# First modulation by feature tiles with three QKV units abreast; later modulation in two norm passages, last head turned inside the output projection, bias loads on SP

## Chip, cores and metric

The kernel runs on one core of one Trainium2 chip. The time is that of one execution on the device, in microseconds; of several runs the median counts.

## What is computed

Two blocks one after the other on 256 tokens of width 1024, in float32. Only the first block is touched here. It has two layers and a second stream of 256 context tokens that passes through the first layer too.

```python
silu_c, silu_cc = jax.nn.silu(c), jax.nn.silu(c_ctx)
for i in range(DEPTH):                       # DEPTH = 2
    sh1, sc1, g1, sh2, sc2, g2 = jnp.split((silu_c @ ada_w[i] + ada_b[i])[:, None, :], 6, axis=-1)
    csh1, csc1, cg1, csh2, csc2, cg2 = jnp.split(silu_cc @ ada_w[i] + ada_b[i], 6, axis=-1)
    h  = rmsnorm(x,  norm_mix[i]) * (1.0 + sc1)  + sh1
    hc = rmsnorm(xc, norm_mix[i]) * (1.0 + csc1) + csh1
    y, yc = diff_attention(...) if i == 0 else neighbourhood_attention(...)
    x = x + g1 * y
    h2 = rmsnorm(x, norm_ffn[i]) * (1.0 + sc2) + sh2
    x = x + g2 * conv_ffn(h2, ...)           # and the same for xc in layer 0
```

`ada_w[i]` is 1024 x 6144: 24 MB a layer, all of it read to multiply two vectors. `diff_attention` subtracts two softmaxes for each of 8 heads, normalizes each head and projects; `neighbourhood_attention` adds a table of relative biases (`rpb`) to the scores.

## The kernel before

**Layout.** Features lie on the 128 partitions, in 8 tiles of 128; both streams stand side by side, 512 columns a tile (`X`, 256 in layer 1 where only x is left). A product is taken in three float32r parts: operands are split into a high and a low half, and `mm3` (line 516) issues high x high, high x low, low x high. A normalized tile is `NH` and `NL`, a weight unit `WH` and `WL`.

**The weight stream.** All weights come as units of up to 1 MB, in the order of the list KEYS that `unit_orders` (line 143) writes out: ("qkv", l, i), ("wo", l, i), ("up", l, j), ("down", l, c, m) and so on. SP issues them in that order (`load_unit`, line 468) into three buffers `RAW`, unit v into v % 3; a load waits until unit v - 3 has been used. `split_hi` (ACT, two halves) writes `WH`, `split_lo` (VectorE or POOL, two halves, by POOL_EVERY) writes `WL`; `ahead` names the unit that is two further in the split order. Every engine runs its own instructions in the order written.

**Modulation.** A block ("ada", b, k), b from 0 to 5, is 2048 columns of the six vectors of a layer, so three blocks a layer; k runs over the 8 feature tiles of the contraction. `pe_ada` (line 523) multiplies silu(c) and silu(c_ctx) (`CB`) with one 1 MB unit, unsplit, in four products into bank `AB`; the sum is there after all eight k. Then `act_ada_row` copies the bank, `pe_ada_turn` transposes it and `dve_ada` adds the bias into `ADA`; `dve_gain` makes the gains `AMOD`. Block 0 (shift and scale of layer 0) is done at the start. Block 1 is spread over the eight QKV units, one before each; block 2 over the four V units; block 3 over the first eight up units of layer 0; block 4 over the first down units; block 5 over the second half of the up units.

**The norm.** Squares, `pe_sums` (products with a column of ones; POOL adds the first six tiles ahead in `pool_presum`), `dve_mean`, `pool_rsqrt`, the broadcast `pe_rs_rows`, and then tile by tile `dve_scale`, `act_norm` (writes `NH`; shifts a copy for odd tiles) and the low half on VectorE (even tiles) or POOL (odd ones).

**Start, in order.** SP loads SMALL, unit 0, CONST, unit 1, X in two halves with units 2 and 3 between. PE runs block 0 with the sums between, the broadcast, the turn. Then the first QKV unit runs with all its tiles' eight k steps.

**Attention of layer 0** (`pe_diff` and its three siblings) runs 43 steps; in step n job n (a head and a quarter of the queries) does its QK, and older jobs their later stages: exponential at age 1, mix at 3 (`POOL_MIX` names those on POOL), transposes at 4, PV at 5, and for every fourth job the head's norm at ages 8 and 9 on POOL (L1062, L1067), the turn on PE at 10 (L941), `NH` and `NL` of the head at 11. ACT and POOL split wo(0,0) in steps 1 and 2, ACT and VectorE wo(0,1) in step 35. `pe_wo` follows.

**Attention of layer 1** (`pe_na`, 22 steps, pairs p): scores, bias and maximum on VectorE, exponentials on ACT (L1166), scale on POOL (L1200), transposes and PV. The biases of a chunk of four pairs are loaded into `BR` by four DMAs of 256 KB (`act_load_bias`), then POOL writes `BI` from them in two additions (`pool_bias`, L1102). ACT issues chunk 2 in step 4 and chunk 3 in step 8, among its own work.

## Time and profile before

| what | value |
|---|---|
| median of 3 runs | 1737.33 us (1736.33 to 1737.52) |
| the profiled execution | 1738.02 us, its span 1736.1 us |
| PE busy | 1629.7 us, 94% of the span |
| VectorE, ACT, POOL busy | 868.5, 741.3, 540.7 us |
| HBM read | 246.63 MB, 143 GB/s over the span |

### The profile page before, as it was taken

The page shows a single profiled execution, that of the slowest core. Times are in us where ns is not written, and L with a number is a line of the kernel's source. Part 1 is how long each engine was busy: PE and PEld are TensorE (multiplying, and loading weights), DVE is VectorE, ACT ScalarE, POOL GpSimd, SP SyncE. Part 2 cuts the span into 40 slices and gives each one's busy share as a digit, 9 for nine tenths or more (in the row PEclk, how much of TensorE's full clock was granted, in tenths as well). Part 3 has the DMA queues.
Part 4 walks back from the last instruction along what each step waited for, and adds up shares of the span by engine and source line. Part 5 has one row for each costly group of instructions (what it writes and reads, how often), then busy time and mean ns, then how long its engine had stood idle before and what let it go on. Part 6 is the DMA issues. An engine that isn't in the chain of part 4 may idle for free.

```text
span 1736.1 us, 26371 instructions
## 1 busy us (share of the span) xinstructions
PE 1629.7 (94%) x10864; PEld 1414.9 (81%) x10864; DVE 868.5 (50%) x1367; ACT 741.3 (43%) x1332; POOL 540.7 (31%) x362
## 2 busy tenths in 40 slices
PE   4999876999999999989978999999999999999997
PEld 1778654877777777878955899999999998999997
DVE  2642376345532355343145588747466454568434
ACT  2421376243422233333246555534654444554442
POOL 2321244222211122211326111104433555523553
PEclk9999999989999999989989999999999999999998
DMA  8543500234436344324321455454534553633551
GB/s 337 182 182 127 213 1 25 73 140 152 155 128 238 116 152 156 99 81 136 138 83 26 149 175 190 145 196 139 191 122 154 186 170 116 214 122 122 184 185 45
DMA packets 52903, 249.38 MB, mean 144 GB/s; under 512 B 20656, under 2 KB 21680, under 8 KB 26288
## 3 DMA queue, kind: packets, MB, share of 16 engines
q1 hardware_dynamic: 36000, 242.32, 39.7%
q10 hardware_dynamic: 16784, 5.38, 1.4%
q8 instruction: 86, 1.41, 0.3%
q14 instruction: 33, 0.27, 0.0%
HBM read 246.63 MB, written 1.05 MB: 143 GB/s over the span
## 4 chain that ended last, share of the span: by engine, by line
PE 88%; DVE 4%; POOL 3%; issue 2%; ACT 1%; DMA 1%; SPq 0%; POOLq 0%; DVEq 0%; ACTq 0%
PE psq L518 20%; PE psq L519 19%; PE psq L520 19%; PE ps L518 6%; PE ps L520 6%; PE ps L519 6%; PE ps L531 3%; DMA RAW<-wstream 1%; DVE STAT L1019 1%; PE psq L969 1%; PE psq L1835 1%; PE ps L626 1%; PE ps L668 1%; PE ps L1126 1%; PE psq L1139 1%
## 5 line engine op out<-in xcount | busy, mean ns | idle before, releaser
L518 PE MATMUL psq<-NH,WH 128*128 128x256 f32 (+1 forms) x1904 | 602.4, 316 | 20.1 <-POOL NL L2159 5.9
L519 PE MATMUL psq<-NL,WH 128*128 128x256 f32 (+1 forms) x1904 | 594.2, 312 | 0.0
L520 PE MATMUL psq<-NH,WL 128*128 128x256 f32 (+1 forms) x1904 | 593.6, 312 | 0.0
L500 DVE TENSOR_TENSOR WL<-RAW,WH 128x1024 fp32r<-128x1024 f32 (+2 forms) x265 | 315.8, 1216 | 459.9 <-ACT WH L490 459.9
L500 POOL TENSOR_TENSOR WL<-RAW,WH 128x1024 fp32r<-128x1024 f32 (+2 forms) x115 | 288.0, 2506 | 597.5 <-ACT WH L490 597.4
L490 ACT ACTIVATE WH<-RAW 128x1024 fp32r<-128x1024 f32 (+2 forms) x380 | 361.2, 1001 | 221.4 <-DMA RAW<-wstream 177.7
L518 PEld LDWEIGHTS psq<-NH,WH 128*128 128x128 f32 x1904 | 369.7, 194 | 59.8 <-issue 27.1
L520 PEld LDWEIGHTS psq<-NH,WL 128*128 128x128 f32 x1904 | 369.9, 194 | 18.7
L519 PEld LDWEIGHTS psq<-NL,WH 128*128 128x128 f32 x1904 | 370.2, 194 | 17.7
L1414 POOL TENSOR_TENSOR HL<-TMP,HH 128x512 fp32r<-128x512 f32 (+1 forms) x44 | 45.5, 1033 | 247.8 <-ACT HH L1343 134.1
L518 PE MATMUL ps<-NH,WH 128*128 128x256 f32 (+1 forms) x368 | 122.5, 333 | 0.0
L520 PE MATMUL ps<-NH,WL 128*128 128x256 f32 (+1 forms) x368 | 121.9, 331 | 0.0
L519 PE MATMUL ps<-NL,WH 128*128 128x256 f32 (+1 forms) x368 | 121.8, 331 | 0.0
L588 ACT ACTIVATE TMP<-X 128x256 f32<-128x256 f32 (+1 forms) x52 | 24.8, 496 | 154.5 <-DVE X L1233 112.0
L518 PEld LDWEIGHTS ps<-NH,WH 128*128 128x128 f32 x368 | 70.4, 191 | 12.1 <-issue 5.0
L520 PEld LDWEIGHTS ps<-NH,WL 128*128 128x128 f32 x368 | 70.4, 191 | 6.5
L519 PEld LDWEIGHTS ps<-NL,WH 128*128 128x128 f32 x368 | 70.3, 191 | 6.2
L1392 DVE SCALAR_TENSOR_TENSOR TMP<-psq,SMALL,TMP 128x510 f32<-128x510 f32 (+1 forms) x64 | 39.2, 613 | 72.2 <-ACT TMP L1357 71.9
L531 PE MATMUL ps<-RAW,CB 128*32 128x512 f32 x384 | 56.7, 673 | 19.2 <-DMA RAW<-wstream 16.3
L1357 ACT ACTIVATE TMP<-psq,SMALL 128x512 f32<-128x512 f32 (+1 forms) x64 | 40.6, 667 | 79.8 <-PE psq L520 79.8
L611 POOL TENSOR_TENSOR TMP<-TMP 128x512 f32<-128x512 f32 (+1 forms) x30 | 31.0, 1035 | 106.8 <-ACT TMP L588 91.7
L2081 ACT ACTIVATE M<-psq 128x512 f32<-128x512 f32 x32 | 19.1, 598 | 102.0 <-PE psq L520 102.0
(311 smaller groups left out, 2559.8 us busy)
## 6 DMA issues: line engine op xcount, KB each, us to landing
RAW<-wstream SPq DMA_DIRECT2D x204, 1024.0 KB, 4.9
RAW<-wstream SPq DMA_DIRECT2D x32, 704.0 KB, 4.1
BR<-rpb ACTq DMA_DIRECT2D x16, 256.0 KB, 7.8
X<-xin SPq DMA_DIRECT2D x2, 1024.0 KB, 12.7
LATEC<-late ACTq DMA_DIRECT2D x1, 1152.0 KB, 6.1
RAW<-wstream SPq DMA_DIRECT2D x2, 576.0 KB, 4.2
out<-X SPq DMA_DIRECT2D x8, 128.0 KB, 2.1
CONST<-consts SPq DMA_DIRECT2D x1, 542.0 KB, 6.8
```

Of the source, the lines that this page charges most:

```text
L490: e.activation(WH[:, u % 3, a:z], RAW[:, v % 3, a:z], ACT.Copy).then_inc(w_hi, 1)
L500: e.tensor_tensor(WL[:, u % 3, a:z], RAW[:, v % 3, a:z], WH[:, u % 3, a:z].bitcast(F32), ALU.subtract).then_inc(w_lo_p if pool else w_lo_v, 1)
L518: e.matmul(o, lh, rh, start=start, stop=False)
L519: e.matmul(o, lh, rl, start=False, stop=False)
L520: return e.matmul(o, ll, rh, start=False, stop=stop)
L531: mm = e.matmul(AB[32 * j:32 * j + 32, :], CB[:, k, :], RAW[:, v % 3, 512 * j:512 * j + 512], start=k == 0, stop=k == DT - 1)
L588: e.activation(sq_tile(n, m), X[:, m, 0:NORM_T[n]], ACT.Square).then_inc(x_sq, 1)
L611: e.tensor_tensor(sum_tile(n), first, sq_tile(n, m), ALU.add).then_inc(sq_acc, 1)
L1357: e.activation(acc_tile(l, U, s), up_banks(l, jj)[s][:, :], ACT.Identity, scale=small_at("fconv", (3 * l + 1) * 44 + j + FT * s), bias=sma ...
L1392: e.scalar_tensor_tensor(out=a3[:, :, 1:256], in0=o3[:, :, 0:255], scalar=w(0), in1=a3[:, :, 1:256], op0=ALU.mult, op1=ALU.add).then_inc(u ...
L1414: e.tensor_tensor(HL[l][:, jj, :], acc_tile(l, U, 0), HH[l][:, jj, :].bitcast(F32), ALU.subtract).then_inc(h_lo, 1)
L2081: e.activation(M[:, n % 2, 2 * j:2 * j + 2, :], pair(ring_bank(f"m{n}{j}")), ACT.Tanh, scale=0.5).then_inc(m_tanh, 1)
```

## The change

Six edits, of the order and the place of work. (1) Block 0 goes. Shift and scale of layer 0 are computed from an array `first` of eight 1 MB pieces, one for each feature tile: 256 columns with the whole contraction. For tile j, `pe_first` does eight products in four column groups, ACT copies the bank, `pe_first_sel` sums the groups in two small products, VectorE adds the bias and makes the gain, and tile j of the norm follows. The six homes of these loads are Q0, K0 and V0, not yet in use. (2) QKV units 0, 1 and 2 run abreast in six banks, in pieces of one k step, put between the tiles by FIRST_PIECES; X is loaded first, splits of QKV run three units ahead, and the sums of norm 0 take all eight tiles on PE. (3) Block 1 runs behind units 3 to 7; block 2, with its row and turn, in steps 0 to 9 of attention; the splits of wo(0,0) and wo(0,1) move to steps 34 and 36. (4) Blocks 3 and 5: units 0 to 2 between the last sums of the norm ahead, 3 and 4 behind its broadcast, 5, 6 and 7 before the next three units. (5) The last head's turn moves into wo's sixth k step. (6) Bias chunks 2 and 3 are issued by SP behind the load of wo(1,3); the split of wo(1,1) moves to steps 17 and 18, and a one-element exponential stands in front of the last two V units' work on ACT.

The new order and functions, cut:

```diff
+    late_ada = iter(range(DT))
+    for i in range(8):
+        add(("qkv", 0, i), 1 if i < 3 else 2)
+        for _ in range((0, 0, 0, 2, 2, 2, 1, 1)[i]):
+            k = next(late_ada)
+            add_ada(1, k)
+            run_ada(1, k)
...
+UP_ADA = {("up", 0, 0): (0, 1, 2, 3, 4), ("up", 0, 1): (5,), ("up", 0, 2): (6,), ("up", 0, 3): (7,)}
+QKV_ADA = {("qkv", 1, 4): (0, 1, 2, 3, 4), ("qkv", 1, 5): (5,), ("qkv", 1, 6): (6,), ("qkv", 1, 7): (7,)}
...
+        def pe_first(e, j):
...
+            e.wait_ge(d_first[j % 6], 16 * (j // 6 + 1))
+            for k in range(DT):
+                s = 32 * (k % 4)
+                mm = e.matmul(AB[s:s + 32, 0:256], CB[:, k, :], HOMES[j % 6][:, 256 * k:256 * k + 256], start=k < 4,
+                              stop=k >= 4)
+            mm.then_inc(f_mm, 1)
+        def pe_first_sel(e, j):
+            e.wait_ge(d_const, 16)
+            e.wait_ge(f_row, j + 1)
+            for p in range(2):
+                mm = e.matmul(AB[:, 256 + 2 * p:258 + 2 * p], TMP[:, 9, P * p:P * p + P], const_at("sel", 0, 2), start=True,
+                              stop=True)
+            mm.then_inc(f_sel, 1)
...
+        FIRST_PIECES = (([], []), ([], [(0, 0)]), ([(0, 1)], [(1, 0), (1, 1)]), ([(0, 2)], [(1, 2)]),
...
-                if n in (2, 35):
-                    split_hi(e, SPLIT_AT[UNIT_OF["wo", 0, 0 if n == 2 else 1]])
+                if n in (34, 36):
+                    split_hi(e, SPLIT_AT[UNIT_OF["wo", 0, (n - 34) // 2]])
...
-                if n == 1:
+                if n == 34:
                     split_lo(e, SPLIT_AT[UNIT_OF["wo", 0, 0]], True)
...
-                if n in (4, 8):
-                    act_load_bias(e, 2 if n == 4 else 3)
+                if n == 17:
+                    split_hi(e, SPLIT_AT[UNIT_OF["wo", 1, 1]])
...
+        def pe_wait_heads(e, k):
+            if k == 5:
+                pe_out_turn(e, 7)
+            e.wait_ge(o_lo, k + 1)
...
+            for v, js in enumerate(((0, 1), (2, 3), (4, 5, 6, 7))):
                 load_unit(e, v)
...
+                for j in js:
+                    load_first(e, j)
+            for v in range(3, NU):
+                load_unit(e, v)
+                if KEYS[v] == ("wo", 1, 3):
+                    load_bias(e, 2)
+                    load_bias(e, 3)
```

**PE at the start.** Rows of one kind that follow each other are counted (x24 is six units). Before, L531 is a modulation unit's product, L626 a sum, L668 the broadcast, L546 the turn, L518 to L520 the three parts of a QKV product:

```order
L531 MATMUL ps7<-RAW,CB 32x512 x24
L626 MATMUL ps6<-CONST,TMP 128x1 x12
L531 MATMUL ps7<-RAW,CB 32x512 x4
L668 MATMUL ps6<-CONST,RS 128x128 x4
L531 MATMUL ps7<-RAW,CB 32x512 x4
L546 MATMUL ps7<-CONST,TMP 128x128 x4
L531 MATMUL ps7<-RAW,CB 32x512 x4
```

Now, with L665 a sum, L579 a tile's products, L593 its select, L707 the broadcast, L520 to L522 the parts of a QKV product:

```order
L665 MATMUL ps6<-ONES,TMP 128x1 x32
L579 MATMUL ps7<-K0,CB 32x256 x8
L593 MATMUL ps7<-CONST,TMP 128x2 x2
L707 MATMUL ps6<-CONST,RS 128x128 x4
L579 MATMUL ps7<-K0,CB 32x256 x8
L593 MATMUL ps7<-CONST,TMP 128x2 x2
L520 MATMUL psq<-NH,WH 128x512
L521 MATMUL psq<-NL,WH 128x512
L522 MATMUL psq<-NH,WL 128x512
```

The first QKV products follow two tiles of modulation instead of a whole block and a unit; the sums stand first.

**PE in the norm behind the first output projection.** Before:

```order
L520 MATMUL psq<-NH,WL 128x512
L626 MATMUL ps6<-CONST,TMP 128x1 x12
L668 MATMUL ps6<-CONST,RS 128x128 x4
L531 MATMUL ps7<-RAW,CB 32x512 x4
L518 MATMUL psq<-NH,WH 128x512
```

Now, where L533 is a modulation unit's product:

```order
L522 MATMUL psq<-NH,WL 128x512
L665 MATMUL ps6<-ONES,TMP 128x1 x4
L533 MATMUL ps7<-RAW,CB 32x512 x4
L665 MATMUL ps6<-ONES,TMP 128x1 x4
L533 MATMUL ps7<-RAW,CB 32x512 x4
L665 MATMUL ps6<-ONES,TMP 128x1 x4
L533 MATMUL ps7<-RAW,CB 32x512 x4
L707 MATMUL ps6<-CONST,RS 128x128 x4
L533 MATMUL ps7<-RAW,CB 32x512 x8
L520 MATMUL psq<-NH,WH 128x512
```

Three units stand ahead of the broadcast, two of them ahead of the last sum, and two behind it.

**ACT in the attention of layer 1.** Before, L490 is the high half of a weight split, L1166 the exponentials, L1095 the bias load, L1152 the copies of the transposes:

```order
L490 ACTIVATE WH<-RAW 128x1024 x2
L1166 ACT_TABLE_LOAD
L1166 ACTIVATE PA,STAT<-psq,STAT 128x512 x4
L1166 ACTIVATE TMP,STAT<-psq,STAT 128x512 x2
L1095 DMA BR<-rpb 64x16x64 x4
L1152 ACTIVATE TMP<-ps4 128x512
L1152 ACTIVATE TMP<-ps5 128x512
```

Now ACT has the table load two V units earlier and no loads here (L492 split, L915 a V copy, L918 the one-element exponential, L1221 exponentials):

```order
L918 ACT_TABLE_LOAD
L918 ACTIVATE STAT<-ONES 128x1
L492 ACTIVATE WH<-RAW 128x1024 x2
L915 ACTIVATE V1<-ps4 128x2x256
L915 ACTIVATE V1<-ps5 128x2x256
L1221 ACTIVATE PA,STAT<-psq,STAT 128x512 x4
L1221 ACTIVATE TMP,STAT<-psq,STAT 128x512 x2
```

The loads stand on SP between the unit wo(1,3) and the up units of layer 1.

## Rows read from the trace of the kernel before

**Rows 1.** The page's chain that ended last: share of the span by engine.

```profile
PE 88%; DVE 4%; POOL 3%; issue 2%; ACT 1%; DMA 1%; SPq 0%; POOLq 0%; DVEq 0%; ACTq 0%
```

**Rows 2.** Timeline, PE, start: start us, us, instruction, [idle before <- who ended it].

```profile
23.38 1.87 PE L531 MATMUL ps<-RAW,CB 128*32 128x512 f32 x8 [0.55 <-DMA RAW<-wstream]
...
25.87 1.07 PE L531 MATMUL ps<-RAW,CB 128*32 128x512 f32 x8 [0.62 <-DMA RAW<-wstream]
...
26.86 3.85 PE L626 MATMUL ps<-CONST,TMP 128*128 128x1 f32 x24
...
43.80 0.79 PE L518 MATMUL psq<-NH,WH 128*128 128x512 f32 x1 [4.99 <-DVE WL L500]
```

**Rows 3.** Timeline, layer 0's attention, its entry and its end.

```profile
206.00 5.11 POOL L500 TENSOR_TENSOR WL<-RAW,WH 128x1024 fp32r<-128x1024 f32 x2 [19.91 <-ACT WH L490]
...
206.47 2.42 DVE L1029 SCALAR_TENSOR_TENSOR PP<-PP,STAT 128x512 f32<-128x512 f32 x1
...
219.34 0.75 DVE L1029 SCALAR_TENSOR_TENSOR PP<-PP,STAT 128x512 f32<-128x512 f32 x1
...
293.74 1.04 POOL L1067 TENSOR_TENSOR TMP<-TMP,STAT 128x512 f32<-128x512 f32 x1
...
302.28 1.11 PE L941 MATMUL ps<-CONST,TMP 128*128 128x128 f32 x4 [6.53 <-POOL TMP L1067]
```

**Rows 4.** Timeline, PE, the norm behind the first output projection.

```profile
353.38 2.07 PE L668 MATMUL ps<-CONST,RS 128*128 128x128 f32 x8 [1.35 <-POOL RS L663]
...
358.08 0.77 PE L518 MATMUL psq<-NH,WH 128*128 128x512 f32 x1 [0.77 <-DVE NL L719]
```

**Rows 5.** Busy us by stretch: length, PE, PEld, DVE, ACT, POOL, granted clock, DMA.

```profile
202.00:205.00 3.00, 1.13 (x4) 0.30 (x4) 0.80 (x3) 2.87 (x10) 0.00 (x0) 1.00 1.01 423
205.00:208.00 3.00, 1.29 (x8) 0.72 (x8) 2.93 (x4) 3.00 (x6) 2.00 (x1) 1.00 0.15 63
...
224.00:256.00 32.00, 25.12 (x156) 15.79 (x157) 23.56 (x60) 23.67 (x85) 16.21 (x16) 1.00 0.00 1
...
361.00:364.00 3.00, 3.00 (x10) 2.34 (x10) 2.94 (x8) 2.90 (x8) 1.79 (x3) 0.67 0.96 407
...
588.00:592.00 4.00, 4.00 (x11) 3.15 (x12) 0.00 (x0) 0.00 (x0) 0.00 (x0) 0.57 0.74 248
```

**Rows 6.** Timeline, PE, second half of the feed-forward, and layer 1's QKV begin.

```profile
586.88 1.06 PE L531 MATMUL ps<-RAW,CB 128*32 128x512 f32 x8 [2.58 <-issue]
...
767.72 0.77 PE L518 MATMUL psq<-NH,WH 128*128 128x512 f32 x1 [2.63 <-DVE NL L719]
```

**Rows 7.** Timeline, layer 1's attention (ACTq: issues on ACT's queue).

```profile
884.50 2.36 DVE L500 TENSOR_TENSOR WL<-RAW,WH 128x1024 fp32r<-128x1024 f32 x2 [9.15 <-ACT WH L490]
...
891.27 2.04 POOL L1200 TENSOR_TENSOR PA<-PA,STAT 128x512 f32<-128x512 f32 x2 [26.32 <-DVE STAT L1186]
...
913.64 5.05 ACTq L1095 DMA_DIRECT2D BR<-rpb  x3
...
925.05 2.35 POOL L1102 TENSOR_TENSOR BI<-BR,CONST 128x1024 f32<-128x1024 f32 x1 [6.09 <-DMA BR<-rpb]
...
928.46 0.66 PE L1115 MATMUL ps<-CONST,TMP 128*128 128x128 f32 x4 [2.62 <-POOL TMP L1200]
```

**Rows 8.** Timeline, PE, QKV of layer 0: units of modulation, turn, first scores.

```profile
82.89 1.07 PE L531 MATMUL ps<-RAW,CB 128*32 128x512 f32 x8
...
94.99 1.07 PE L531 MATMUL ps<-RAW,CB 128*32 128x512 f32 x8
...
144.73 0.66 PE L546 MATMUL ps<-CONST,TMP 128*128 128x128 f32 x4 [1.24 <-ACT TMP L539]
...
199.61 1.56 PE L969 MATMUL psq<-K,Q 64*128 64x512 f32 x8
```

**Rows 9.** Groups by line and shape, 35 to 83 us: busy us, mean ns, idle.

```profile
L732 POOL TENSOR_TENSOR NL<-TMP,NH 128x256 fp32r<-128x256 f32 x8 | 7.6, 964 | 8.5 <-ACT TMP L711 8.5
```

**Rows 10.** The page's DMA issues: KB each, median us from issue to landing.

```profile
RAW<-wstream SPq DMA_DIRECT2D x204, 1024.0 KB, 4.9
```

More of the change, by code:

```diff
@@ L195, in unit_orders @@
         add(("qkv", 1, i), 1000)
+        if i == 5:
+            for k in range(DT):
+                add_ada(5, k)
+    for name, at, b in (("up", UP_ADA, 3), ("qkv", QKV_ADA, 5)):
+        for key, ks in at.items():
+            r = runs.index(key)
+            runs[r:r] = [("ada", b, k) for k in ks]
     for i in range(8, 12):
@@ L308 @@
 NORM_AT = {n: a for a, n in enumerate(NORM_T)}
-PRESUM = {n: 0 if n == 5 else 6 for n in NORM_T}
+PRESUM = {n: 0 if n in (0, 5) else 6 for n in NORM_T}
 SUMS = {n: DT - PRESUM[n] + (1 if PRESUM[n] else 0) for n in NORM_T}
@@ L568, in sum_tile @@
         def sum_tile(n):
-            return TMP[:, 8 if n == 0 else 6, 0:NORM_T[n]]
+            return TMP[:, 6, 0:NORM_T[n]]
         def wait_sq_taken(e, n, m):
@@ L806, in pe_qkv @@
             n = 2 * l
+            late_ada = iter(range(DT))
             for u, i in enumerate(QKV_ORDER[l]):
                 b = qk_slot(u)
-                if l == 0:
-                    pe_ada(e, 1, i)
+                if l == 0 and u < 3:
+                    continue
                 if u >= 3:
                     e.wait_ge(qk_sb, qk_outputs_before(l, u - 2))
+                if l == 1:
+                    for k in QKV_ADA.get(("qkv", 1, i), ()):
+                        if k > 2:
+                            pe_ada(e, 5, k)
+                    if u == 6:
+                        pe_ada_turn(e, 5)
                 wait_x = (lambda k: pe_wait_norm(e, n, k)) if u == 0 else nothing
@@ L817, in pe_qkv @@
                     pe_wide(e, ("qkv", l, i), [bank[b][:, :], bank[b + 1][:, :]], 512, NH, NL, wait_x, u == 0)
+                if l == 0:
+                    for _ in range((0, 0, 0, 2, 2, 2, 1, 1)[i]):
+                        pe_ada(e, 1, next(late_ada))
             for i in range(4):
                 b = qk_slot(8 + i)
-                if l == 0 and i == 0:
+                if l == 0 and i == 1:
                     pe_ada_turn(e, 1)
-                elif l == 0:
-                    pe_ada(e, 2, 2 * i - 2)
-                    pe_ada(e, 2, 2 * i - 1)
                 if i < 3:
@@ L860, in act_qkv @@
                     act_ada_row(e, 1)
+                if l == 1 and u == 4:
+                    act_ada_row(e, 5)
             for i in range(4):
@@ L867, in act_qkv @@
                                  ACT.Copy).then_inc(v_sb, 1)
-                if l or i < 2:
+                if l == 1 and i == 2:
+                    e.activation(STAT[:, 11, 16:17], ONE, ACT.Exp)
+                if i < 3 if l else i == 0:
                     split_hi(e, ahead(key))
@@ L886, in dve_qkv @@
                     e.tensor_tensor(dst[:, m, 0:256], dst[:, m, 0:256], s, ALU.add).then_inc(rot_v, 1)
-            if l == 0:
-                dve_ada(e, 1)
-            for i in range(4 if l else 2):
+            dve_ada(e, 1 if l == 0 else 5)
+            for i in range(3 if l else 1):
                 split_lo(e, ahead(("qkv", l, 8 + i)), False)
@@ L903, in pool_qkv @@
                 pool_bias(e, 1, 1)
-            for i in range(4 if l else 2):
+            for i in range(3 if l else 1):
                 split_lo(e, ahead(("qkv", l, 8 + i)), True)
@@ L928, in wait_mix, with pe_out_turn @@
                 e.wait_ge(mix_v, j + 1 - p)
+        def pe_out_turn(e, h):
+            e.wait_ge(o_norm, h + 1)
+            if h == 0:
+                e.wait_ge(ada_par, 2)
+            else:
+                e.wait_ge(o_lo, h)
+            for q in range(4):
+                mm = e.transpose(AB[:, q * P:q * P + P], TMP[:, 7 + h % 2, q * P:q * P + P], IDENT)
+            mm.then_inc(o_tr, 1)
         def pe_diff(e):
@@ L1219, in pe_wo @@
                         pe_sums(e, n, m)
+            if l == 0:
+                pe_ada(e, 3, 0)
             pe_sums(e, n, 6)
+            if l == 0:
+                pe_ada(e, 3, 1)
             pe_sums(e, n, 7)
+            if l == 0:
+                pe_ada(e, 3, 2)
         def act_wo(e, l):
@@ L2453, in dve_start @@
                 e.tensor_reduce(LAMV[:, 2 + j:3 + j], t, AX, ALU.add, negate=False).then_inc(lam_v, 1)
+            dve_mean(e, 0)
+            split_lo(e, 0, False)
+            for j in range(DT):
+                dve_first(e, j)
+                dve_scale(e, 0, j)
+                if j % 2 == 0:
+                    dve_norm_lo(e, 0, j)
+                if j in (1, 3):
+                    split_lo(e, (j + 1) // 2, False)
             e.wait_ge(lam_exp, 1)
@@ L2721, in layout @@
         "wstream": pack_weights(v),
+        "first": pack_first(v),
         "small": small,
```

268 lines of the change are left out of this document (136 added, 132 removed).

## Prediction

> **What bounds the kernel now.** I read the chain of waits first: TensorE (PE) has 88% of it [rows 1], so a term counts only where it takes work or idle time off PE. Next, PE's idle gaps in order of time: 43.8 us pass before the first product of QKV [rows 2]; the attention of layer 0 ends in a gap of 6.5 us behind POOL [rows 3]; the norm behind the first output projection runs at a low clock [rows 4, 5]; up(0,13) waits 2.58 us behind a modulation block [rows 6]; and in the neighbourhood attention of layer 1 ACT issues DMAs and POOL waits for them [rows 7]. In each place I ask what ends last there. A "unit of modulation" is one `pe_ada`: 1 MB of weights, one x8 row, 1.0 us of PE where the clock is high. In QKV a pair of output tiles and one such unit come every 12.1 us [rows 8], so a pair is 11.1, and one of its eight k steps (a "piece", six products) 1.39.
>
> **The start, tile by tile.** Loads land 2.49 us per 1024 KB [rows 2]; by 25.87 SMALL, CONST and 8 MB had come, 8.96 units, so the stream began at 3.6. In the new queue f0 (the first feature tile's weights) stands behind X, SMALL, CONST and one QKV unit: 3.6 + 4.96 x 2.49 = 15.9; f1 lands at 18.4, f2 at 23.4, f3 25.9, f4 30.8, the rest at 33.3, 35.8 and 38.3. On PE: the sums are now 64 instructions at 0.16 us (24 took 3.85 [rows 2]), since POOL no longer adds ahead: 10.3, from 6.8 (first X at 6.1, a square) to 17.1. f0's products cost what a unit does, as they stream the same columns in all: 1.9 at the low clock [rows 2], to 19.0. Copy and select take 1.2 (estimate: a 0.4 copy, four loads at the sums' 0.16, hand-overs), to 20.2; the row broadcast 2.07 [rows 4], to 22.3; f1 and its select end at 25.5. From there 24 pieces x 1.39, six tiles' products x 1.07 [rows 8] and six selects x 0.65 make 43.7 us: 69.2. To this come waits. From a select to a tile's NL is 3.0 us for an even tile (2.6 from the broadcast's end to the first product [rows 4], 0.4 for addition and gain) and about 4 for an odd one, whose two halves POOL does at 0.96 [rows 9]. PE asks for tiles 1, 3 and 7 some 2.5 us after their select: 3 x 1.5; and 1 us for the low clock at the first pieces. The three units end at 74.7. Unit 3's weights can be split only when unit 0 has ended, and its banks be emptied: 1 us more, 75.7. Before, unit 3 began at 83.9 [rows 8]: 8.2 gained. Behind that point 4 units of block 1 and 8 of block 2 followed, now 8 of block 1: 4.0 gained. The 1.24 us wait at the turn [rows 8] goes, as the turn stands one unit later. **Start: -13.4**; bounds -19.6 (no waits) and -1 (B, below).
>
> **Block 2 in attention.** One unit stands behind each of steps 0 to 7. PE has room there: 3.6 us idle in 202 to 208, and later 6.9 in 32 [rows 5], 2.4 in the 11 us of steps 4 to 7. Without the split on POOL the first mix takes 0.75, not 2.42, so step 4 begins 1.7 earlier [rows 3]. That is 7.7 of room for 8 units: I take their cost as 0.3, and up to 8 if that cover fails, where the mixes' chain is late next. The loads follow: three are there at the start, each later one is issued when the unit three before it is done, two to three steps ahead of its use. Row copy and turn move into full steps: 0.5. **+0.8.**
> What the row shows at the entry is a mix of 2.42 us beside POOL's split, 0.75 without it [rows 3]. The Trainium skill's SBUF — State Buffer page (SBUF: two separate sides) calls the port pair that VectorE and GpSimd share "an **exclusive lock**, not a bandwidth split". By it the split's new place also holds VectorE's split of wo(0,1), up to 2.5 us a half; that is wanted 11 us later, so the sum would be the same, and no run here shows it yet.
>
> **End of attention.** The split of wo(0,0) now stands on POOL behind its last mix and ahead of head 6's scale: 5.11 us [rows 3]. Half a microsecond of it fills a gap; with ACT's split ahead, head 6's scale, at 293.74 before, comes near 300.1, its turn ends at 301.9, and wo begins at 302.0, not 303.0 [rows 3], because it needs no more than that turn. Head 7's turn (0.66) runs inside wo, five pieces later: hidden but for its own time. What is late next is POOL. **-0.4**; bounds -6.5 (the whole gap) and +5 (the whole split).
>
> **Norm behind wo.** Before, one unit lay in the passage and 7 on the path; now 5 and 3 (two of the five behind the broadcast, where PE waits for NL): -4.0. Two units stand ahead of the last sum, so the broadcast starts 2.1 later than 353.38. If the clock falls as before, -1.9. If it stays up, the broadcast takes 1.2 and the low stretch from 358.08 to about 363, worth 2.4, is gone [rows 4, 5]: -5.1. **-3.0.**
>
> **Block 5.** Eight units leave the second half of the feed-forward; 5 go into the norm passage, 3 stay on the path: -5.0. The 2.58 us wait [rows 6] goes, and the low clock behind it (0.57 of 4 us [rows 5]): -1.7. Against it, unit 4 can be loaded only when unit 1 is done, at 762.9, and lands 4.9 later [rows 10], as QKV would start [rows 6]: +0.3; the broadcast is later, +0.9, or with the clock up -2.4 in its place. **-9.5**; bounds -8 and -11.5.
>
> **Neighbourhood attention.** The split of wo(1,1) leaves VectorE's queue (2.36 from 884.50 [rows 7]), and the exponential's table is loaded earlier: masks begin at 884.3, and POOL's first scale comes 2.5 earlier, at 888.8 [rows 7]. The first moved load (chunk 2) is issued on SP behind wo(1,3), near 877, and has landed when POOL wants it. The second waits for `bias_sb` 6, for POOL's two chunk 2 additions: four scales of 2.04 and two additions of 2.35 from 888.8, and 0.3 of waits, end at 902.0. From issue to use it takes 12 us (its issues begin 0.6 ahead of 913.64, the addition at 925.05 [rows 7]): 914.1. POOL needs 2.4 and 1.0 to the next half pair, so PE goes on at 917.5 against 928.46. The wait at chunk 3 stays, and is what is late next. SP's queue behind it holds the up weights of layer 1, not wanted for 40 us. ACT's split at step 17 stands ahead of its copies: +1. **-10**; bounds -8 and -11.7.
>
> **The sum.** -13.4 + 0.8 - 0.4 - 3.0 - 9.5 - 10.0 = -35.5, against the profiled execution's 1738.0 (span 1736.1, the rest outside it): 1702.5. The median of the runs shown is 0.7 lower, so I predict 1701.8. The terms' bounds, not all at one end, give 1692 to 1711.
>
> **Rivals.**
> A, the forecast: 0.60.
> B, the chain of one tile bounds the start. By my rows it is 6.3 us (products 1.1, copy and select 1.2, NL 4); if ACT's splits and POOL's stretch it to 8, the chain gives 17.1 + 8 x 8 + 7 for the last pieces = 88, 12.3 more than 75.7 allows: 1714; 0.17. For it: three splits of unit weights stand among ACT's copies. Against it: pieces of other tiles stand between.
> C, the clock stays up. Norm -5.1, block 5 -11.5; at the start, first products, broadcast and first pieces at full speed are worth up to 5, I take 3: 1701.8 - 2.1 - 2.0 - 3.0 = 1694.7; 0.17. For it: no gap over 2 us is left in the passages. Against it: right behind the sums the broadcast took 2.07 [rows 4].
> The Trainium skill's TensorE: Matmul & The Clock Gate (What's actually happening) has "the default state is throttled, and activity releases the throttle"; by that C would be the case.
> D, slower: the ring of three RAW buffers. Block 1's units now stand in pairs, and a load is issued only when the unit three back is used. From the first of a pair to the next weights it takes 3 loads, 2.4 fixed (4.9 [rows 10] less 2.49) and 2.25 for splits: 12.1 of the 14.1 that there are. If each load takes 4.9 in turn, 19.4: 5.3 short, and 2.3 more for the clock that such a gap costs [rows 4, 5]. Six units (4 to 8, and 10): +45, 1747. It decides the sign above 4.4 us a load. Against it: loads queued back to back land every 2.49 [rows 2]. 0.04.
> The last 0.02 is spread: a moved step that is held up somewhere else.
>
> **How the numbers follow.** 1701.8 is A. The range takes in A's bounds, B and C: 1686 to 1719. Faster by over 0.2% (3.5 us, about what a measurement here tells from no change): A, B and C, 0.94. Within 0.2%: 0.01. Slower: D and half of the rest, 0.05.
>
> **What would show it.** Unit 3's first product at 74 to 77; QK of job 0 near 186; wo's first product some 103 us behind it, as before; POOL's split of wo(0,0) right ahead of two short pow steps; five units in each norm passage with no gap over 1.5 us; one wait of POOL for BR, about 6 us, instead of two. I am wrong if unit 3 starts past 84, if units in QKV or attention wait for RAW, or if POOL no longer waits for BR.

## The result and the profile after

The changed kernel takes 1707.11 us (median of 4 runs, 1705.45 to 1707.67); before stands at 1737.08 in the same comparison. The ratio is 0.9825, with a 95% interval of 0.9810 to 0.9839: 30 us faster. The forecast was 1701.8 with a range of 1686 to 1719, so it lies inside, 5.3 us above the forecast: 30.0 of the 35.5 us came. The profiled execution is the shortest of the four, 1705.45 with a span of 1703.6: 32.5 us less span than before. In two of the experiments below one of four executions took far longer (3274.76 and 4012.73 us), and their ratios are those of the other three.

The page after has this busy time and this chain that ended last:

```profile
PE 1623.3 (95%) x10996; PEld 1421.4 (83%) x10996; DVE 874.5 (51%) x1382; ACT 743.6 (44%) x1341; POOL 540.6 (32%) x358
...
PE 87%; DVE 3%; POOL 3%; DMA 3%; issue 2%; ACT 2%; POOLq 0%; DVEq 0%; SPq 0%; ACTq 0%
```

PE's work fell by 6.4 us only (1629.7 before); the other 26 of the 32.5 are idle time that went. New in the chain is DMA with 3%, where it had 1% [rows 1].

To see where the time went, I take the same product in both traces and subtract its starts. Each stage runs from one such product to the next.

| stage | before | after | gained | forecast |
|---|---|---|---|---|
| start to the first scores of layer 0 | 199.61 | 188.57 | 11.0 | 13.4 |
| first scores to output projection | 103.43 | 102.67 | 0.8 | -0.4 |
| projection, norm passage, to the last unit of block 3 | | | 4.4 | 3.0 |
| block 5 and QKV of layer 1, to its first scores | | | 8.0 | 9.5 |
| attention of layer 1, to its output projection | 72.25 | 64.78 | 7.5 | 10.0 |
| the rest, to the last product | 768.82 | 768.05 | 0.8 | 0 |

The stages in the middle have no length of their own in the table, because units moved across their borders; there the offset between the two traces is -11.8 at the output projection, -16.2 behind block 3 and -24.2 at the first scores of layer 1.

**Start.** Timeline of PE (start, us, instruction, [idle before <- who ended it]):

```profile
6.52 13.78 PE L665 MATMUL ps<-ONES,TMP 128*128 128x1 f32 x64 [6.52 <-ACT TMP L630]
20.23 1.93 PE L579 MATMUL ps<-K,CB 128*32 128x256 f32 x16
...
28.96 0.77 PE L520 MATMUL psq<-NH,WH 128*128 128x512 f32 x1
...
44.91 0.50 PE L520 MATMUL psq<-NH,WH 128*128 128x512 f32 x1 [1.43 <-POOL NL L775]
...
72.36 0.50 PE L520 MATMUL psq<-NH,WH 128*128 128x512 f32 x1 [1.05 <-POOL NL L775]
...
77.28 0.50 PE L520 MATMUL psq<-NH,WH 128*128 128x512 f32 x1 [0.50 <-ACT TMP L905]
```

The first product comes at 28.96 instead of 43.80 [rows 2]. The 64 sums last until the first tile's products at 20.23, 0.215 us each. Among the pieces only those of tiles 3 and 7 wait for their low half (1.43 and 1.05 us). Unit 3 begins at 77.28; before, it began behind the unit of modulation of 82.89 [rows 8].

**End of layer 0's attention.** POOL, then VectorE, then PE:

```profile
282.65 4.66 POOL L502 TENSOR_TENSOR WL<-RAW,WH 128x1024 fp32r<-128x1024 f32 x2 [1.39 <-ACT WH L492]
...
289.34 1.08 POOL L1122 TENSOR_TENSOR TMP<-TMP,STAT 128x512 f32<-128x512 f32 x1
...
285.35 4.17 DVE L502 TENSOR_TENSOR WL<-RAW,WH 128x1024 fp32r<-128x1024 f32 x2 [2.12 <-ACT WH L492]
...
290.47 1.11 PE L987 MATMUL ps<-CONST,TMP 128*128 128x128 f32 x4 [5.63 <-POOL TMP L1122]
291.24 0.77 PE L520 MATMUL psq<-NH,WH 128*128 128x512 f32 x1
```

POOL's split stands ahead of head 6's norm, and PE waits 5.63 us; before it waited 6.53 for the last head's norm [rows 3].

**Norm passages.** PE, first behind the projection, then ahead of layer 1's QKV:

```profile
341.20 1.05 PE L665 MATMUL ps<-ONES,TMP 128*128 128x1 f32 x8
...
343.61 1.16 PE L707 MATMUL ps<-CONST,RS 128*128 128x128 f32 x8 [0.36 <-POOL RS L700]
...
347.95 1.07 PE L533 MATMUL ps<-RAW,CB 128*32 128x512 f32 x8 [2.19 <-DMA RAW<-wstream]
348.95 0.50 PE L520 MATMUL psq<-NH,WH 128*128 128x512 f32 x1
...
738.32 1.06 PE L533 MATMUL ps<-RAW,CB 128*32 128x512 f32 x8 [1.66 <-DMA RAW<-wstream]
739.31 0.50 PE L520 MATMUL psq<-NH,WH 128*128 128x512 f32 x1
```

The broadcast takes 1.16 us instead of 2.07 [rows 4], and the first product 0.50 instead of 0.77: the clock stayed up, and 8 sums take 1.05 us (0.13 each). But the fifth unit waits for its weights, 2.19 and 1.66 us.

**QKV of layer 1.** VectorE, POOL and PE near 762:

```profile
762.55 5.92 DVE L502 TENSOR_TENSOR WL<-RAW,WH 128x1024 fp32r<-128x1024 f32 x2 [17.56 <-ACT WH L492]
...
761.70 5.68 POOL L1157 TENSOR_TENSOR BI<-BR,CONST 128x1024 f32<-128x1024 f32 x2 [14.72 <-DMA BR<-rpb]
...
765.20 0.50 PE L520 MATMUL ps<-NH,WH 128*128 128x512 f32 x1 [1.62 <-DVE WL L502]
```

A split that takes 2.36 us alone [rows 7] takes 5.92 beside POOL's bias additions, and PE waits 1.62 (and 0.30 once more behind it). This belongs to this profile: in the eight others whose code is the same here, PE waits 0 to 0.58 us for that split.

**Attention of layer 1.** POOL's one wait for BR, what PE did around it, and PE's waits at the end:

```profile
891.01 2.35 POOL L1157 TENSOR_TENSOR BI<-BR,CONST 128x1024 f32<-128x1024 f32 x1 [6.00 <-DMA BR<-rpb]
...
887.88 1.09 PE L1181 MATMUL ps<-TMP,V 128*64 128x128 f32 x16
888.90 1.13 PE L1194 MATMUL psq<-K,Q 64*128 64x512 f32 x4
894.41 2.11 PE L1170 MATMUL ps<-CONST,TMP 128*128 128x128 f32 x8 [4.39 <-POOL TMP L1257]
896.46 1.98 PE L1181 MATMUL ps<-TMP,V 128*64 128x128 f32 x16
898.37 1.72 PE L1194 MATMUL psq<-K,Q 64*128 64x512 f32 x4
900.02 1.09 PE L1170 MATMUL ps<-CONST,PA 128*128 128x128 f32 x8
...
918.25 1.11 PE L1170 MATMUL ps<-CONST,TMP 128*128 128x128 f32 x8 [1.64 <-ACT TMP L1207]
...
923.11 1.09 PE L1181 MATMUL ps<-TMP,V 128*64 128x128 f32 x16 [0.67 <-DVE NL L1247]
```

One wait of 6.00 us is left of the two of before. Behind it the gap costs twice: 4.39 us of standing, and 2.5 us more because the next three groups (5.81 us) run at the low clock; at the high one they take 1.09, 1.09 and 1.13. At the end PE waits 1.64 us for ACT's copy behind the split of (wo, 1, 1), and 0.67 for a low half on VectorE.

### The profile page after: what moved, and what is told of

It reads as the page before. It is cut to its first block, busy times and chain, and to the rows that moved or that the text cites. A ratio compares the mean times of both kernels' runs of the same rounds, so it can differ in the third digit from the quotient of the medians.

```text
span 1703.6 us, 26688 instructions
## 1 busy us (share of the span) xinstructions
PE 1623.3 (95%) x10996; PEld 1421.4 (83%) x10996; DVE 874.5 (51%) x1382; ACT 743.6 (44%) x1341; POOL 540.6 (32%) x358
## 3 DMA queue, kind: packets, MB, share of 16 engines
q8 instruction: 87, 1.43, 0.3%
HBM read 246.63 MB, written 1.05 MB: 145 GB/s over the span
## 4 chain that ended last, share of the span: by engine, by line
PE 87%; DVE 3%; POOL 3%; DMA 3%; issue 2%; ACT 2%; POOLq 0%; DVEq 0%; SPq 0%; ACTq 0%
PE psq L520 19%; PE psq L521 19%; PE psq L522 19%; PE ps L520 6%; PE ps L522 6%; PE ps L521 6%; DMA RAW<-wstream 2%; PE ps L533 2%; PE ps L665 1%; PE psq L1022 1%; PE psq L1905 1%; DVE STAT L1074 1%; PE ps L579 1%; PE ps L1002 0%; DVE WL L502 0%
## 5 line engine op out<-in xcount | busy, mean ns | idle before, releaser
L520 PE MATMUL psq<-NH,WH 128*128 128x256 f32 (+1 forms) x1904 | 600.2, 315 | 13.6 <-POOL NL L2229 5.0
L522 PE MATMUL psq<-NH,WL 128*128 128x256 f32 (+1 forms) x1904 | 592.0, 311 | 0.0
L502 DVE TENSOR_TENSOR WL<-RAW,WH 128x1024 fp32r<-128x1024 f32 (+3 forms) x264 | 322.9, 1247 | 387.2 <-ACT WH L492 387.2
L502 POOL TENSOR_TENSOR WL<-RAW,WH 128x1024 fp32r<-128x1024 f32 (+2 forms) x116 | 292.2, 2521 | 533.7 <-ACT WH L492 533.6
L492 ACT ACTIVATE WH<-RAW 128x1024 fp32r<-128x1024 f32 (+2 forms) x380 | 361.1, 1001 | 194.1 <-DMA RAW<-wstream 151.7
L520 PEld LDWEIGHTS psq<-NH,WH 128*128 128x128 f32 x1904 | 368.6, 194 | 45.9 <-issue 19.6
L522 PEld LDWEIGHTS psq<-NH,WL 128*128 128x128 f32 x1904 | 368.7, 194 | 18.2
L521 PEld LDWEIGHTS psq<-NL,WH 128*128 128x128 f32 x1904 | 369.2, 194 | 17.1
L520 PE MATMUL ps<-NH,WH 128*128 128x256 f32 (+1 forms) x368 | 121.9, 331 | 2.5 <-DVE WL L502 1.9
L522 PE MATMUL ps<-NH,WL 128*128 128x256 f32 (+1 forms) x368 | 121.1, 329 | 0.0
L630 ACT ACTIVATE TMP<-X 128x256 f32<-128x256 f32 (+1 forms) x52 | 24.8, 497 | 139.2 <-DVE X L1304 102.7
L520 PEld LDWEIGHTS ps<-NH,WH 128*128 128x128 f32 x368 | 70.0, 190 | 12.5 <-DVE WL L502 3.3
L522 PEld LDWEIGHTS ps<-NH,WL 128*128 128x128 f32 x368 | 70.0, 190 | 6.4
L520 PE MATMUL psq<-HH,WH 128*128 128x512 f32 (+1 forms) x176 | 60.3, 343 | 0.0
L520 PE MATMUL ps<-HH,WH 128*128 128x512 f32 (+1 forms) x176 | 60.2, 342 | 0.0
```

The lines of the kernel that those rows point to most:

```text
L492: e.activation(WH[:, u % 3, a:z], RAW[:, v % 3, a:z], ACT.Copy).then_inc(w_hi, 1)
L502: e.tensor_tensor(WL[:, u % 3, a:z], RAW[:, v % 3, a:z], WH[:, u % 3, a:z].bitcast(F32), ALU.subtract).then_inc(w_lo_p if pool else w_lo_v, 1)
L520: e.matmul(o, lh, rh, start=start, stop=False)
L521: e.matmul(o, lh, rl, start=False, stop=False)
L522: return e.matmul(o, ll, rh, start=False, stop=stop)
L630: e.activation(sq_tile(n, m), X[:, m, 0:NORM_T[n]], ACT.Square).then_inc(x_sq, 1)
```

## The experiments

Each is the changed kernel with one edit. The same code gave stages of somewhat different length from profile to profile: the first scores at 187.9 to 189.7, the attention of layer 0 in 102.7 to 105.7, that of layer 1 in 63.2 to 64.8 (eight profiles in each case, of kernels that leave the stage alone). A stage is read against these ranges, a whole run by its ratio to before, 0.9825 for the changed kernel. GpSimd is POOL.

### The sums of the first norm

```diff
+PRESUM[0] = 4      # POOL adds the squares of tiles 5, 6 and 7 to those of tile 4
-            for m in range(DT):
-                pe_sums(e, 0, m)
+            for m in range(5):
+                pe_first_sums(e, m)
```

> The changed kernel, except that GpSimd adds the squares of the last four feature tiles of the first norm, so that TensorE sums five operands instead of eight (40 short products instead of 64). Theory S (those sums at 0.215 us each hold the start): they end near 15.1 us instead of 20.23, the first tile's modulation starts when its weights have landed, near 16.6, the first QKV product comes near 25.3 instead of 28.96, and the time falls by some 3.5 us, to 1703.6. Rival B (the chain of a tile, or its weights, sets the start): the first QKV product comes earlier but the fourth QKV unit stays within 1 us of 77.3, and the time stays at 1707 +- 1.

Measured: the first scores came at 182.76, 5.8 us earlier than in the changed kernel's profile. PE's start:

```profile
6.43 8.75 PE L2528 MATMUL ps<-ONES,TMP 128*128 128x1 f32 x40 [6.43 <-ACT TMP L630]
15.69 1.94 PE L579 MATMUL ps<-K,CB 128*32 128x256 f32 x16 [0.51 <-DMA K<-first]
...
23.89 0.47 PE L520 MATMUL psq<-NH,WH 128*128 128x512 f32 x1
```

The sums end at 15.2, 5.1 us earlier, then the weights of the first tile are what is waited for (0.51 us), as expected. The first product gains 5.07 us and not the 3.7 expected, mainly because those weights land at 15.7 and not at 16.6. It runs at the high clock already (0.47 against 0.77 us). Rival B is out: the gain reaches the first scores whole. Of the whole run less is seen (0.9821, 0.9801 to 0.9841): the profiled execution gained 4.0, but the runs lie at 1701.6, 1704.9 and 1707.1; the edit on four units comes back to such spreads.

### The split of the first output projection unit

```diff
 KEYS: ("wo", 0, 0) ahead of the units of block 2
-                if n in (34, 36):
+                if n == 36:                 # only ("wo", 0, 1) is split here
-                if n == 34:                 # POOL's low half of ("wo", 0, 0)
-                    split_lo(e, SPLIT_AT[UNIT_OF["wo", 0, 0]], True)
+ACT and VectorE split ("wo", 0, 0) behind the second V unit
```

> The changed kernel, except that the first output projection unit is loaded ahead of block 2 and split by ACT and VectorE during the V units, before the attention of layer 0, instead of by ACT and GpSimd at its end. Theory P (GpSimd's split of 4.66 us stands ahead of head 6's norm and makes the gap of 5.63 us): head 6's turn comes near 285 instead of 290.5, the output projection starts there at the high clock, and the time falls by 5.4 to 7 us, to some 1701. Rival (the end of attention is set by the heads' own chain and by the split of the second unit): less than 1.5 us is gained, and up to 2 us are lost in the V units, where ACT now splits between its copies: 1706 to 1709.

Measured: 1701.38 us (0.9795, 0.9780 to 0.9810), and an attention of 95.80 us against 102.7 to 105.7. POOL, then PE:

```profile
283.58 1.04 POOL L1124 TENSOR_TENSOR TMP<-TMP,STAT 128x512 f32<-128x512 f32 x1
...
285.00 0.60 PE L989 MATMUL ps<-CONST,TMP 128*128 128x128 f32 x4
285.36 0.48 PE L522 MATMUL psq<-NH,WH 128*128 128x512 f32 x1
```

No gap is left and the clock stays up. Theory P holds: POOL's split was all of the gap. The projection's fourth product stands 7.7 us ahead of the changed kernel's; the profiled execution gave back 6 of them later, among them 2.0 at a low clock when QKV of layer 1 begins, while the median kept 5.7.

### The last head's turn

```diff
-                    if age == 10 and qt == 3 and h < 7:
+                    if age == 10 and qt == 3:
-            if k == 5:
-                pe_out_turn(e, 7)
```

> The changed kernel with one edit undone: the last head's turn stands again ahead of the output projection of layer 0. Theory (the turn inside hides the last head's chain, whose norm ends at 295.4 where the projection now starts at 291.2): the projection's first product comes near 296.1 and the time rises by 4.9 us, to 1712. Rival (the projection's sixth step waits for the last head anyway, so that only the turn's 0.6 us shows): 1707.7.

Measured: 1713.08 us (0.9854, 0.9839 to 0.9869). PE:

```profile
293.25 1.12 PE L987 MATMUL ps<-CONST,TMP 128*128 128x128 f32 x4 [5.63 <-POOL TMP L1122]
298.21 1.12 PE L987 MATMUL ps<-CONST,TMP 128*128 128x128 f32 x4 [3.84 <-POOL TMP L1122]
298.98 0.78 PE L520 MATMUL psq<-NH,WH 128*128 128x512 f32 x1
```

The projection starts 5.7 us behind head 6's turn, where the changed kernel needs 0.8: the edit is worth 5.0 us. The net -0.4 of the forecast was thus a gain of 5.0 against the cost of POOL's split that moved into the same place: 4.7 us by its length, 6.9 by what the attention gained without it.

### Block 2 in the attention

```diff
+                if l == 0 and i >= 2:       # among the V units
+                    pe_ada(e, 2, 2 * i - 4)
+                    pe_ada(e, 2, 2 * i - 3)
...
+                pe_ada(e, 2, 4)             # behind the last one
+                pe_ada(e, 2, 5)
-                if n < DT:
-                    pe_ada(e, 2, n)
+                if n < 2:
+                    pe_ada(e, 2, 6 + n)
```

> The changed kernel with six of the eight units of block 2 taken out of the attention of layer 0 and put back among the V units (two ahead of the third, two ahead of the fourth, two behind it); the last two stay in steps 0 and 1. Theory (the units are free in the attention, as the prediction has it at +0.3 for eight): the V units take 6 x 0.97 = 5.8 us longer and the attention is as long as now (102.7 us from the first scores to the output projection): 1712.9. Rival (there they cost what they do elsewhere): the attention is shorter by as much, 1707 +- 1.

Measured: first scores at 193.68 (5.1 later), an attention of 102.52 us, 1711.43 us in all (0.9844, 0.9829 to 0.9858). The attention is as long as the shortest of the same code when six units leave it (102.67 in the changed kernel's profile), and without them PE stands idle. So they cost nothing there as long as their weights come in time. Where a unit waits longer the attention is longer, up to 105.7 us, and six units fewer may spare some of that: by its ratio the whole run is some 3 us longer than the changed kernel, not 5, with intervals that overlap. A wait of PE in the first steps, without the units:

```profile
202.65 1.02 PE L1021 MATMUL ps<-CONST,PP 128*128 128x128 f32 x4 [2.09 <-DVE PP L1095]
```

### The bias loads

```diff
+                if n in (4, 8):             # ACT again
+                    load_bias(e, 2 if n == 4 else 3)
-                if KEYS[v] == ("wo", 1, 3): # on SP
-                    load_bias(e, 2)
-                    load_bias(e, 3)
```

> The changed kernel with one edit undone: the bias loads of chunks 2 and 3 stand on ACT again, in steps 4 and 8. Theory N (the loads are what the attention of layer 1 gained by): GpSimd waits some 8 us for chunk 2 again, and that attention, from its first scores to the second output projection, takes 70 to 72 us instead of 64.8 (72.3 in the kernel before): 1712 to 1714. Rival (the split that left VectorE's queue and the table loaded early made the gain): 66 to 67 us, 1708 to 1709.

Measured: 71.44 us for that attention and 1715.14 in all (0.9863, 0.9849 to 0.9878). POOL waits twice again:

```profile
880.98 2.37 POOL L1157 TENSOR_TENSOR BI<-BR,CONST 128x1024 f32<-128x1024 f32 x1 [6.85 <-DMA BR<-rpb]
...
899.74 2.35 POOL L1157 TENSOR_TENSOR BI<-BR,CONST 128x1024 f32<-128x1024 f32 x1 [6.09 <-DMA BR<-rpb]
```

Against the 63.2 to 64.8 us of the same code the loads are worth 6.6 to 8.2 us, so nearly all of the 7.5; what the split that left VectorE's queue and the table loaded early add is lost in that spread.

### A second place for the bias

```diff
+            if qt == 1:                     # bias_at, for chunk 3
+                return BR[:, 0, :, :]
+            return TMP[:, 8:10, :].rearrange("p a (b c) -> p (a b) c", c=64)
...
+                if ch == 3:
+                    if r == 2:
+                        e.wait_ge(bias_sb, 5)
```

> The changed kernel, except that the bias of chunk 3 is loaded half into a free place (tiles 8 and 9 of TMP) at once and half into the first half of BR as soon as the first addition of chunk 2 has read it. Theory N (one buffer BR makes GpSimd wait 6.0 us, TensorE stands for 4.39 us behind it and then runs 5.8 us at the low clock): the wait and the gap go, the clock stays up, and the neighbourhood attention is 4.4 + 2.5 = 6.9 us shorter: 1700.2. Rival (GpSimd's own work is as late: 32 scales and 8 additions): the gap of 4.39 us turns into several small ones and the time falls by less than 2 us.

Measured: 58.03 us, 6.75 less, and 1701.24 in all (0.9792, 0.9778 to 0.9807). POOL's additions of chunk 3 wait for nothing:

```profile
885.90 2.36 POOL L1176 TENSOR_TENSOR BI<-TMP,CONST 128x1024 f32<-128x1024 f32 x1
...
890.21 2.37 POOL L1176 TENSOR_TENSOR BI<-BR,CONST 128x1024 f32<-128x1024 f32 x1
```

Theory N holds with its number (6.9): the one buffer cost a gap and a stretch at the low clock. The stretch is not equally long in all profiles: from the sixth to the eighth of the 16 products with V the one buffer cost 6.0 to 6.7 us in nine.

### The split of (wo, 1, 1)

```diff
-                if n == 17:
-                    split_hi(e, SPLIT_AT[UNIT_OF["wo", 1, 1]])
-                if i < 3 if l else i == 0:
+                if l or i == 0:             # behind the last V unit
-                if n == 18:
+                if n == 17:
                     split_lo(e, SPLIT_AT[UNIT_OF["wo", 1, 1]], False)
```

> The changed kernel, except that ACT's half of the split of unit (wo, 1, 1) stands behind the last V unit, before the attention of layer 1, and VectorE's half one step earlier, in step 17. Theory T (the moved split is what the end of that attention waits for: 1.64 us for ACT's copy behind it, 0.67 us for VectorE's low half): both waits go and the time falls by 2.3 us, to 1704.8. Rival (those waits are the pipeline running empty, and ACT's split at the front delays the first exponentials instead): 1706.5 to 1708.

Measured: 63.93 us, within 63.2 to 64.8 of the same code, and 1707.01 in all (0.9816, 0.9800 to 0.9833). Theory T falls in its size. The two waits are gone from the trace, but the pipeline's last steps wait 1.43 us for other engines:

```profile
923.57 0.66 PE L1170 MATMUL ps<-CONST,TMP 128*128 128x128 f32 x4 [0.71 <-POOL TMP L1255]
924.95 1.97 PE L1181 MATMUL ps<-TMP,V 128*64 128x128 f32 x32 [0.72 <-ACT TMP L1205]
```

From the twelfth of the 16 products with V to the projection it takes 9.86 us here and in the run of all five edits, and 10.66 or 10.67 in the ten profiles that have the split in step 17: the edit is worth 0.8 of the 2.3 us, too little to show in the whole run. I had taken the name on a wait for its price.

### The order of the loads in QKV of layer 1

```diff
-            for k in range(DT):
+            for k in range(DT - 1):
                 add_ada(5, k)
+        if i == 6:
+            add_ada(5, DT - 1)
```

> The changed kernel, except that the last unit of block 5 is loaded behind the QKV unit (1, 6) instead of ahead of it. Theory O (that unit's weights come late, at 761.5, because their buffer is held by unit 5 of block 5; their split then meets the bias additions on GpSimd and takes 5.92 instead of 2.36 us): the weights land near 745 to 750, both splits are done before the additions, the waits of 1.62 and 0.30 us at 765 and 768 go, and the time falls by 1.9 us, to 1705.2. Rival (the bias load of 1 MB in small pieces holds up whatever is loaded beside it): the split moves, but the next unit waits instead; 1707 +- 0.7.

Measured: the waits of 1.62 and 0.30 us are gone, and from QKV's first product to the first scores of layer 1 it takes 118.61 us against 120.04. That is not shown to be the edit's doing: in the eight other profiles with the old order these waits are 0 to 0.58 us, and the stretch takes 118.9 to 121.7. Theory O priced a place that was late in one profile. The whole run shows nothing, 0.9832 (0.9815 to 0.9848). In the profile QKV began 2 us later: the fifth unit had waited 2.01 us, and the clock fell. That led to the runs that follow.

### Four units in a passage, and the changed kernel again

```diff
-UP_ADA = {("up", 0, 0): (0, 1, 2, 3, 4), ("up", 0, 1): (5,), ...
+UP_ADA = {("up", 0, 0): (0, 1, 2, 3), ("up", 0, 1): (4,), ("up", 0, 2): (5,), ("up", 0, 3): (6, 7)}
 QKV_ADA alike; block 5 loaded 0 to 4 behind (1, 5), 5 behind (1, 6), 6 and 7 behind (1, 7); block 3 likewise
```

> The changed kernel again, beside the next two on the same chip. Theory C (the clock is marginal in the second norm passage: it fell there in four profiles of five when the last unit of block 5 ahead of QKV waited over 2 us for its weights, and it stayed up in the profile of the changed kernel, where that wait was 1.66): this profile shows the wait and the clock together, either under 2 us and QKV's first product 0.50 us long, or over 2 us and 0.80 us long; the times spread over 2 to 3 us round 1707.

> The changed kernel with four units instead of five in each norm passage; the fifth runs ahead of the second unit behind it, two run ahead of the fourth, and the loads are ordered to match (QKV's units no longer stand behind all eight). Theory C (the fifth unit waits for its weights, 2.19 and 1.66 us, behind the broadcast, and that wait decides the clock; the QKV unit (1, 6) comes late because its buffer is held): the passages end when the first tile's low half is there, 1.5 and 2.0 us earlier, the unit costs 1.0 each on the path, the waits of 1.62 and 0.30 us at 765 go, and the clock stays up in every run: 3.4 us less than the profile of the changed kernel, 1702 to 1704 with a spread under 2 us. Rival (the unit was the cover: TensorE now waits for the low half and the clock falls behind it): 1707 to 1710.

The changed kernel again took 1708.48 us (1705.44 to 1710.50; 0.9827, 0.9809 to 0.9845). Its profile, 1708.7 us of span, has the other case. PE in the attention of layer 0 (block 2's fifth unit), and at QKV of layer 1:

```profile
201.92 1.56 PE L533 MATMUL ps<-RAW,CB 128*32 128x512 f32 x8 [2.05 <-DMA RAW<-wstream]
...
742.35 1.94 PE L533 MATMUL ps<-RAW,CB 128*32 128x512 f32 x8 [2.15 <-DMA RAW<-wstream]
744.22 0.80 PE L520 MATMUL psq<-NH,WH 128*128 128x512 f32 x1
```

In both places a unit waits over 2 us for its weights, and what follows runs at the low clock: the attention took 105.69 us. In the profile of the changed kernel the same waits are 0.81 and 1.66 us, and the clock stays up. In the ten profiles with five units ahead of QKV the wait is 1.66 to 2.72 us; the clock fell in nine of them, from 2.01 us up, and stayed up at 1.66 alone. A fall there cost 1.6 to 2.9 us. In the first passage the waits are as long, 1.17 to 2.74 us, and the clock fell behind one of them only (2.66). In three of twelve profiles it had fallen ahead of it, while PE did not wait at all: the third unit took 1.82 to 1.91 us and the broadcast 1.94 to 2.03 (granted clock 0.62 from 345 to 348 us in the changed kernel's second profile, with PE busy for all of the 3 us). So a wait goes with the fall in the one passage, but does not decide it alone; what does is open. In the second passage the fourth unit waits too, 0.89 to 1.21 us, in the first in one profile only (0.39); no run tells whether that is the difference.

With four units the fifth's waits are gone, and PE waits for the low half of the first tile instead, as expected:

```profile
349.91 0.47 PE L518 MATMUL psq<-NH,WH 128*128 128x512 f32 x1 [1.64 <-DVE NL L760]
...
739.54 0.47 PE L518 MATMUL psq<-NH,WH 128*128 128x512 f32 x1 [0.35 <-DVE NL L760]
```

1702.86 us (0.9797, 0.9781 to 0.9812): 5.6 us less than the changed kernel beside it. From the first projection to the first scores of layer 1 the profile takes 565.04 us, against 568.1 to 570.3 in the nine with the old code there. Moving a unit onto the path paid, because in the passage it cost its load's delay. The edit also loads the last three units of block 5 later, and its gain is that of both. The clock had been expected to stay up in every run, and did not: this is one of the three profiles with a slow broadcast in the first passage (1.94 us).

### The five edits together

> The changed kernel with five of the edits tried here together: squares of four tiles added on GpSimd, the first output projection unit split before the attention, four units in a passage, a second place for the bias, and ACT's half of the split of (wo, 1, 1) ahead of layer 1's attention. Theory (each place stands by itself, as the profiles of the single edits show: -4.0, -6 to -7.7, -3.4, -6.8, -0.9): 1684 to 1686. Rival (what one place gains is lost where the weights then come late, as the edit of the projection unit lost 4 of its 7.7 us again further on): 1690 to 1693.

Measured: 1682.69 us (1681.39 to 1684.47; 0.968, 0.9664 to 0.9696). The first scores of layer 0 come at 182.81, its attention takes 97.51 us, that of layer 1 57.87. Stage by stage these are the gains of the single edits (182.76, 95.80 and 58.03 us), the attention of layer 0 less 1.7 us; this version beats both kernels, the changed one by some 25 us. It has the edit of (wo, 1, 1) in it, which alone is worth 0.8 us.

## Why the prediction was right, and where its sizes were off

**Start, -13.4; measured -11.0.** The step that failed is the sums: 64 at the 0.16 us of [rows 2] gave 17.1 for their end, and it was 20.23, since each took 0.215. The 0.16 was a mean over a stretch in which the clock fell. Before, the unit ahead of the 24 sums took 1.07 us [rows 2], the one behind them nearly twice that:

```profile
30.65 1.93 PE L531 MATMUL ps<-RAW,CB 128*32 128x512 f32 x8
```

The edit on the sums showed that they were on the path. The term for waits was too large, 4.5 against the 2.5 us that tiles 3 and 7 show, and hid part of it: unit 3 started at 77.28 against 75.7, 0.3 past the 74 to 77 named as the sign. Behind it the four units and the turn came off as worked out, but 0.56 us for a bank at 103.89 and 0.69 for a V copy at 188.57 were not in the sum. Rival B did not occur.

**Block 2 in attention, +0.8.** The cover is real: with the clock up, six units out give no time back. What I got wrong is the loads: "two to three steps ahead of its use" is not enough for the fifth unit, which waits 0.5 to 2.05 us in the profiles (0.81 in the changed kernel's, and the fourth 0.57). So one of the signs of being wrong, units that wait for RAW in attention, came. That is rival D's mechanism, the ring of three buffers, in a place where I had not looked for it and at a small part of its price. In QKV, where I had it, no unit waited.

**End of attention, -0.4; measured within the spread.** Right for its own reason: POOL's split is what is late. Two large terms, -5.0 for the turn and +4.7 to +6.9 for the split, nearly cancel; the two experiments show each. A net this small is not resolved by stages that differ by 3 us from profile to profile.

**Norm behind wo, -3.0; measured -4.4 (-3.3 to -6.1 in other profiles).** The clock stayed up, as in the -5.1 of the second case, and the 2.19 us of the fifth unit's load took part of it back. The forecast had worked out such a load for block 5 alone, at +0.3, with a landing time of 4.9 us; the trace shows 1.66 to 2.72 of waiting. The sign "no gap over 1.5 us" was wrong. Rival C was half right: in this profile the clock stays up in both passages and is low at the start, but the twelve profiles of this study show both levels for the same instructions (the broadcast 1.16 or some 2 us). By the page TensorE: Matmul & The Clock Gate of the Trainium skill (What's actually happening) activity releases the throttle. The rows of the start agree, where a product takes 0.63 us at 29.54 and 0.39 at 33.51. They do not bear out rival C's use of it, that a passage without gaps keeps the clock: in three profiles it fell in the first passage while PE did not wait (third unit 1.82 to 1.91 us).

**Block 5, -9.5; measured -8.0 (-4.2 to -8.0 in other profiles).** The 2.58 us stall went, as said. Not foreseen: the fifth unit's wait, and in this profile 1.92 us where the late weights of (1, 6) put VectorE's split beside POOL's additions (5.92 us instead of 2.36). The Trainium skill's SBUF — State Buffer (SBUF: two separate sides) calls the shared port pair an exclusive lock; the row agrees, and so does the 4.17 us of VectorE's split beside POOL's at the end of attention. The prediction had that rule in its hand for the one place and not for the other.

**Neighbourhood attention, -10.0; measured -7.5 (to -9.0 in other profiles).** One wait of 6.0 us stayed, as forecast. PE goes on behind it 35.06 us after the first scores, where before it was 44.88: 9.8 earlier, and 11.0 had been worked out, since POOL's first scale came 2.0 and not 2.5 us earlier, counted from the first scores, and its next ones waited 1.2 and not 0.3. The low clock behind the gap is not what is missing: the forecast had no term for it, but before, the groups behind the wait of 2.62 [rows 7] were slow too, and from that wait to the second product with V behind it takes 6.6 us now and took 6.3.

```profile
930.43 1.97 PE L1126 MATMUL ps<-TMP,V 128*64 128x128 f32 x16
```

The term that was too small is the last one, +1 for ACT's split at step 17. From the twelfth of the 16 products with V to the projection it takes 10.66 us now and took 8.67, so it was 2.0: PE waits 1.64 and 0.67. Moving the split gave back 0.8.

**The sum.** Between the two profiled executions, the longest before and the shortest after, 32.5 of 35.5 came; by the medians 30.0. The parts were off by more than the sum: three stages (start, block 5, attention of layer 1) fell 6.4 us short and the other three gave 3.4 more than forecast, and that these cancel in part is luck. The median is 1.7 us worse than the profiled execution. A likely reason is the low clock behind a late unit: the changed kernel's other profiled execution (1710.50 us) has it, and of the ten profiles with five units ahead of QKV only the changed kernel's first kept the clock there. The other runs have no trace. The forecast had no term for it.

## What to carry to other kernels

Price a short instruction at the clock that it will run at: a sum took 0.13 us at the high one and 0.215 at the low, and a mean of 0.16 over both misled; 64 of them stood at the head of the path. A gap of some us on TensorE costs more than its length, since what follows may run at half speed (4.39 us were worth 6.75), so a wait that stays deserves a second buffer even when it is "only" what is left. Work that fills a gap must have its data there: of five units in a row on three buffers the fifth waited for its load, and four were better than five.
